# Place of the split weights in on-chip memory, and the order of a few steps, in a two-block transformer kernel

## The reference

```python
u = rms_norm(h, attn_norm[l])
proj = einsum('bsd,dc->bsc', u, w_in[l])          # 7424 columns
dq, dk, dv, rq, rk, rv, rg, gq, gk, gv, gate_logits = split_cols(proj, IN_SPLITS)
lam = exp(sum(lam_q1 * lam_k1)) - exp(sum(lam_q2 * lam_k2)) + lambda_init
a = differential_attention(rope(norm(dq)), rope(norm(dk)), dv, lam)   # 4 heads: softmax - lam * softmax
r = bidirectional_retention(rope(rq), rope(rk), rv, ...)              # 4 heads: scores * decay
c = grouped_query_attention(rope(norm(gq)), rope(norm(gk)), gv)       # 8 query heads, 2 key heads
merged = sum(sigmoid(gate_logits) * stack([a, r, c]) @ w_branch[l])
h = h + merged @ w_out[l]
h = h + square(relu(rms_norm(h) @ w_mlp_in[l])) @ w_mlp_out[l]
```

## Time and profile before

| what | value |
| --- | --- |
| median of 3 runs | 3566.72 us (3562.89 to 3567.04) |
| the profiled execution, its own time | 3565.11 us |
| its span in the trace | 3563.3 us (1.8 us lie around it) |
| granted clock of PE, mean (1.00 is 2.4 GHz) | 0.994 |
| PE busy | 3455.9 us, 97% of the span |
| DVE busy | 1744.8 us, 49% |
| ACT busy | 1377.2 us, 39% |
| transfers of the main queue | 308.18 MB, 30.8% of the DMA engines' span |

### The profile page before, as it was taken

One profiled execution on the slowest core, in us unless ns is written; L12 is line 12 of the kernel. 1 busy time (PEld: TensorE's weight loads), 2 busy tenths in 40 slices (PEclk: granted clock), 3 DMA queues, 4 the chain that ended last, 5 costly groups with the idle time before them and its releaser, 6 DMA issues.

```text
span 3563.3 us, 46888 instructions
## 1 busy us (share of the span) xinstructions
PE 3455.9 (97%) x17777; PEld 2705.9 (76%) x17777; DVE 1744.8 (49%) x2520; ACT 1377.2 (39%) x2048; POOL 6.2 (0%) x13
## 2 busy tenths in 40 slices
PE   8998999999999989999999899999999999999999
PEld 5565788788876657887888776588888886579998
DVE  6675434433466754344434557543323355844334
ACT  5554323322246643233222334533323334543334
POOL 0000000000000000000000000000000000000000
PEclk9999999999999999999999999999999999999999
DMA  4121233555541212335565310022222222023332
GB/s 129 52 67 51 80 97 104 148 159 151 149 104 53 64 51 80 98 111 148 153 179 159 83 56 3 2 60 65 61 64 65 59 74 73 4 58 91 94 94 89
DMA packets 577229, 310.26 MB, mean 87 GB/s; under 512 B 28400, under 2 KB 569024, under 8 KB 577088
## 3 DMA queue, kind: packets, MB, share of 16 engines
q1 hardware_dynamic: 576816, 308.18, 30.8%
q10 hardware_dynamic: 272, 0.13, 0.0%
HBM read 297.26 MB, written 2.10 MB: 84 GB/s over the span
## 4 chain that ended last, share of the span: by engine, by line
PE 90%; DVE 5%; ACT 3%; issue 1%; DMA 1%; SPq 0%; DVEq 0%; ACTq 0%
PE ps L1127 14%; PE ps L1129 14%; PE ps L1128 14%; PE ps L1436 11%; PE ps L1438 10%; PE ps L1440 10%; PE ps L1637 2%; PE ps L1317 2%; PE ps L1286 2%; PE ps L1211 1%; PE ps L1298 1%; PE ps L1571 1%; DVE cacc L2955 1%; PE ps L1314 1%; PE ps L1292 1%
## 5 line engine op out<-in xcount | busy, mean ns | idle before, releaser
L1798 ACT ACTIVATE whi<-wraw 128x1024 fp32r<-128x1024 f32 x448 | 470.7, 1052 | 545.8 <-DMA wraw<-in_w_mlp 245.6
L1127 PE MATMUL ps<-uhi,whi 128*128 128x512 f32 (+1 forms) x1456 | 610.3, 419 | 11.9 <-DVE wlo L2436 4.9
L2436 DVE TENSOR_TENSOR wlo<-wraw,whi 128x1024 fp32r<-128x1024 f32 x448 | 545.8, 1219 | 104.7 <-ACT whi L1798 100.1
L1129 PE MATMUL ps<-uhi,wlo 128*128 128x512 f32 (+1 forms) x1456 | 568.8, 391 | 0.0
L1128 PE MATMUL ps<-ulo,whi 128*128 128x512 f32 (+1 forms) x1456 | 564.8, 388 | 0.0
L1127 PEld LDWEIGHTS ps<-uhi,whi 128*128 128x128 f32 x1456 | 274.1, 188 | 94.7 <-issue 37.8
L1128 PEld LDWEIGHTS ps<-ulo,whi 128*128 128x128 f32 x1456 | 274.3, 188 | 68.4 <-issue 16.3
L1129 PEld LDWEIGHTS ps<-uhi,wlo 128*128 128x128 f32 x1456 | 273.8, 188 | 61.7
L1436 PE MATMUL ps<-u2hi,whi 128*128 128x512 f32 (+1 forms) x1216 | 295.1, 319 | 3.7 <-DVE wlo L2436 2.5
L1436 PE MATMUL ps<-yhi,whi 128*128 128x512 f32 (+1 forms) x976 | 295.9, 354 | 0.0
L1438 PE MATMUL ps<-ylo,whi 128*128 128x512 f32 (+1 forms) x976 | 294.0, 352 | 0.0
(11 more groups left out here) (334 smaller groups left out, 4533.7 us busy)
## 6 DMA issues: line engine op xcount, KB each, us to landing
wraw<-in_w_in SPq DMA_DIRECT2D x128, 512.0 KB, 3.8
wraw<-in_w_mlp SPq DMA_DIRECT2D x128, 512.0 KB, 3.9
mod_raw<-in_w_mod SPq DMA_DIRECT2D x96, 512.0 KB, 5.3
wraw<-in_w_mlp_in SPq DMA_DIRECT2D x64, 512.0 KB, 4.2
wraw<-in_w_mlp_out SPq DMA_DIRECT2D x64, 512.0 KB, 3.9
wraw<-in_w_branch SPq DMA_DIRECT2D x16, 512.0 KB, 3.4
wraw<-in_w_out SPq DMA_DIRECT2D x16, 512.0 KB, 3.8
wraw<-in_w_o SPq DMA_DIRECT2D x16, 512.0 KB, 3.8
```

What stands on the lines that cost most here:

```text
L1127: pe.matmul(bank, whs[:, i], x_hi[:, k], start=(i == 0), stop=False)
L1129: last = pe.matmul(bank, wls[:, i], x_hi[:, k], start=False, stop=(i == n - 1))
L1798: act.activation(whi[:, r], wraw[:, r], ACT.Copy).then_inc(w_hi, 1)
L2436: dve.tensor_tensor(wlo[:, r], wraw[:, r], whi[:, r].bitcast(F32), ALU.subtract).then_inc(w_split, 1)
```

## The change

In words, part by part. **Memory:** the arrays `par_mod` and `ident` are handed out ahead of `whi`, so that `whi` begins at byte 2048 and `wraw`/`wlo` at 18432; every slice then begins at a multiple of 512 and none crosses a line of 2048. From `par_dw` on nothing moves, so the activations stay where they are. **PE at the start:** after the last sum of squares 16 products of `ident` with itself into a bank that is overwritten later. **ACT and DVE at the start:** rounding and splitting of chunk 1 are moved behind the root and into the norm; the lambdas are moved behind chunk 2's split. **Heads:** "attended" stands 0.02 instead of 0.4 behind its attend, which moves `bhi`, `blo`, `fsq` and `fo` ahead of other steps on ACT and DVE, in both layers; and the second turn of a gqa unit goes 0.01 behind the next whole part where that part would cut it (one unit in each layer; on PE 8 turns then stand as 4, six products, 4).

```diff
+            first = at + UNIT_SPACE + 0.05
+            piece = math.floor(first) + 1.01
+            second = piece if first + 0.7 < piece < first + 0.84 else first + 0.7
+            for turn in (first, second)[:2 if kind == "gqa" else 1]:
+                s = put(turn, "turn", score=unit, index=int(turn > first))
+                put(turn + 0.3, "turned", head=s, score=unit, index=s.index)
...
-        put(at + 0.4, "attended", head=att)
+        put(at + 0.02, "attended", head=att)
...
+        par_mod = sb("par_mod", [P, 2 * MOD_COLS])
+        ident = sb("ident", [P, P])
         whi = sb("whi", [P, RAW, 1024], F32R)
...
-        ident = sb("ident", [P, P])
         par = sb("par", [P, P])
...
-        par_mod = sb("par_mod", [P, 2 * MOD_COLS])
...
             pe.sem_inc(norm_summed, 1)
+            pe.wait_ge(h_in, KT)
+            for _ in range(16):
+                pe.matmul(ps[:, 0, 0:P], ident[:, :], ident[:, :], start=True, stop=True)
...
-            for chunk in range(2):
-                weight_hi(chunk)
+            weight_hi(0)
...
                 root_of(n.root, n.aux, D, NORM_EPS, (v_ready, n.v + n.tiles))
-
-                if n.chunk:
-                    act.wait_ge(chunk_done, n.chunk)
+                weight_hi(1)
                 for j in range(n.tiles):
...
+                            if step.chunk == 0:
+                                lambdas()
...
-            for chunk in range(LO_AHEAD):
-                weight_lo(chunk)
+            weight_lo(0)
...
+                    if j == 2:
+                        for chunk in range(1, LO_AHEAD):
+                            weight_lo(chunk)
...
                     if step.name == "lo":
                         lo_before(s.norm1.chunk + step.index)
+                        if l == 0 and step.index == 0:
+                            small_lambdas()
```

More of the change, by code:

```diff
@@ L180, in head_schedule @@
             put(at + 1.7, "weigh", score=unit)
-            for m in range(2 if kind == "gqa" else 1):
-                s = put(at + UNIT_SPACE + 0.05 + 0.7 * m, "turn", score=unit, index=m)
-                put(at + UNIT_SPACE + 0.35 + 0.7 * m, "turned", head=s, score=unit, index=m)
+            first = at + UNIT_SPACE + 0.05
[4 more added lines that the diff above has]
+                put(turn + 0.3, "turned", head=s, score=unit, index=s.index)
         at += UNIT_SPACE + 1.45
         att = put(at, "attend", hd=hd, kind=kind, h=part, layer=layer)
-        put(at + 0.4, "attended", head=att)
+        put(at + 0.02, "attended", head=att)
         if kind == "diff":
@@ L1958, in keep_context, with first_norm @@
                     act.activation(context_squares[:, some], hh[:, some, SEQ:ALL], ACT.Square).then_inc(context_squared, 1)
-            def norm(n, between=None):
+            def first_norm(n):
                 act.wait_ge(norm_summed, n.norm + 1)
                 root_of(n.root, n.aux, D, NORM_EPS, (v_ready, n.v + n.tiles))
-                if n.chunk:
-                    act.wait_ge(chunk_done, n.chunk)
+                weight_hi(1)
                 for j in range(n.tiles):
@@ L1968, in norm @@
                     act.activation(uhi[:, j], vst[:, (n.v + j) % 2], ACT.Copy).then_inc(hi_ready, 1)
-                    if between:
-                        between(j)
             act.wait_ge(sq_used, KT)
@@ L1976, in _ @@
                 else:
-                    norm(s.norm1)
+                    first_norm(s.norm1)
                 if s.layer == 0:
@@ L1980, in _, with lambdas @@
                         weight_hi(chunk)
+                def lambdas():
                     act.wait_ge(par_turned, 3)
@@ L2517, in norm_in_halves, with first_norm @@
                     rest(KT - 1)
-            def norm(n, gain):
+            def first_norm(n, gain):
                 inverse_root(n.root)
@@ L2553, in _ @@
                 else:
-                    norm(s.norm1, ROW["attn_norm"] + KT * l)
-                if l == 0:
+                    first_norm(s.norm1, ROW["attn_norm"] + KT * l)
                     small_parameters()
```

1 line of the change is left out of this document (added).

## The result

The change makes the kernel slower. Its median is 3594.52 us (3590.52 to 3596.01, 4 runs), against 3565.4 us before (4 runs): a ratio of 1.0076, with a 95% interval from 1.0063 to 1.0088. The profiled execution took 3590.52 us. Forecast was 3561, between 3552 and 3569.

The account below looks back on a forecast made before the run. PE, holding 90% of the chain that ended last, was taken as the bound. Terms -3.4 + 5.6 - 6.2 - 1.7 - 0.1 = -5.8 us brought 3566.7 to 3561, range 3552 to 3569.

Parts of the forecast that it names:

- Memory: Weight loads and transfers: moving all slices to one offset gives nothing on PE; taken as 0, at most 5.0 us.
- Rival 2: The new memory places do speed something up, 10.8 us per nanosecond per product: 3545 to 3556; 8 in 100.
- Rival 4: Slower: `blo` blocks DVE at the first and third attends too, costing 17.4 and not 5.6: 3573; 8 in 100.
- the first and third attends: gqa attends where `bhi`, `blo` pass a copy, a weigh and a peak: taken as 0, between -0.5 and +0.5.
- The orders: All moved steps outside memory: the terms of start, attends, clock and split turn, summed to -5.8 us.
- The start: Start of the kernel: earlier root and later lambdas let chunk 2 begin earlier on PE; 3.4 us gained, bounds 2.2 to 3.8.
- the 37.4 that was named: Sign at the start: chunk 2 begins on PE near 37.4, with no lambdas ahead of its split.
- The second gqa attend: Weigh and split wait behind `blo`, making a later turn late: 2.8 us lost per layer, 5.6 in both.
- The fourth attend: Fourth gqa attend: earlier `bhi` and `blo` remove PE's wait for the bank; 3.1 us gained per layer, 6.2 in both.
- The lower clock behind the fourth attend: Layer 1, behind the removed wait: 3.3 us at half clock vanish if the pause causes them; 1.7 us gained.
- rival 3: The fourth attend's gain is given back: DVE or ACT late by 3 us, clock falls elsewhere: 3569; 12 in 100.
- The turn's wait for `gw`: Split second turn of a gqa unit removes one wait for `gw`; 0.1 us gained in all, at most 1.6.

Follow-up runs that it names:

- the orders alone: The changed kernel with the old places in memory, so all reordered steps and the 16 products but no memory part: 3561.64 us, ratio 0.998.

## Why the prediction was wrong

**The step that failed** is "Memory": "the offset doesn't show, so moving all to one offset should give nothing on PE". It was worth +33 us by the trace, and 1.0089 by the memory part alone. Two things were wrong in it. It looked at the length of the loads, 188 ns before and after, while the loss is in the distance between products. And its comparison couldn't show anything: the four old offsets of the slices, 128, 640, 1152 and 1664, are all 128 above a multiple of 512, so all slices stood at one and the same distance (192 modulo 256) from the activations. A slice that crosses a line of 2048 bytes costs nothing: at the same distance `uhi` has 229.5 ns before, where a quarter of the slices cross, and 229.4 with weights and `uhi` both moved, where none does. That part of the step was right, but it was not the question. The transfers did become a little faster, 3.6 and not 3.8 us from issue to landing at the median for `w_in`, and nothing came of it: the second block's wait for `wlo` stays at 2.5 us. The trace of before had a hint: `u2hi`, whose rows of 3104 bytes lie at many distances, had steps of 232.9 ns and the other families 229 to 230.

**Rival 2** had the right mechanism and price (one nanosecond per product is 10.8 us), but was only looked at in one direction, as a gain, and so stood inside no range on the slow side. Rival 4, the slow one, did not occur: the first and third attends cost nothing that can be seen.

**The orders** came out as forecast: -5.8 us, and 0.998 [0.997, 0.999] measured, some 7 us. Term by term:

- The start gained 2.7 us between the two executions above (forecast 3.4), because the split of chunk 2 waited 0.81 us for `lag`; with the orders alone there is no such wait, and over all executions it is 3.7. That chunk 2 began at 37.11, near the 37.4 that was named, is chance, since the input came 1.08 us earlier. The prediction took the 16 products as worth nothing and priced them at 2.6 us; they took 3.73, and where they stand there is no lower clock at the first products any more. The time for chunks 0 and 1 stayed, 12.8 us before and 12.9 after, as the prediction had it, but not for its reason: before they ran in part at half the clock, after they wait for slices.
- The second gqa attend lost 3.15 us in layer 0 (22.17 - 19.02) and 2.8 in layer 1, where 2.8 was forecast for each. None of it is the slower products, as it is 22.16 with the orders alone.
- The fourth attend gained 8.25 - 5.24 = 3.0 us (forecast 3.1).
- The lower clock behind the fourth attend has gone, as forecast. In the nine profiled executions without the attended move it begins within 1.5 us of that wait's end in 12 of 18 places, in layer 0 as well as in layer 1, and in the five with the move in none of 10. So it goes with the wait, though it does not come every time. The prediction counted one place of 1.7 us; 12 of them in nine executions are 2.3 us per execution. In the kernel after, 3.4 us of the lower clock stand behind the second attend of layer 1, which cost 1.7 us; rival 3 had a fall elsewhere as a possibility. With the orders alone and with the attended step alone, which have the same waits, it does not occur there.
- The turn's wait for `gw` only moved, 7.9 + 2.7 us in the two rows before and 6.3 + 4.1 after.

One trace shows less than the sum: with the orders alone the last load of `bhi`'s slices in the first block begins at 1998.0 and not 2001.5, 3.5 us earlier. The second block then runs at the lower clock at places that differ from one execution to the next, so a pair of traces doesn't show the whole: over the executions the terms come to 3.7 - 6.0 + 6.0 + 2.3, some 6 us gained.

**What stays open** is why the distance counts. That the load of a slice and the stream of the activations hinder each other is what a dependence on their distance suggests, since the loads run beside the products; but no run here shows it by itself. Nor is it settled why a change from 512 to 256 columns costs `yhi` some 8 ns at distance 0 and under 2 at 192 and 64, and why products of 256 columns go the other way between distances 192 and 64.

## What to carry to other kernels

Where PE streams products back to back, compare the time from start to start by operand, and try the place of one operand against the other in steps of 32 or 64 bytes: here a bad place cost some 30 us and a better one gave 7, for an edit of one or two lines, and a round number was the wrong guess. Before an offset is called harmless, make sure that the offsets compared really differ in what could count. And an early copy out of a bank helps only if what it is moved past does not have to wait with it: the same edit gained 3 us at the one attend and lost 3 at the other.

## What the runs showed of the hardware

In these runs, at the granted clock of 1.00, products of 512 columns in float32r with a load of 128 x 128 each start 227 to 234 ns apart, and it goes with the distance between the two operands in on-chip memory modulo 256 bytes: 227 to 228 at 0, 229 to 230 at 192, 233 to 234 at the other six distances tried (`yhi`, half of whose products are followed by narrower ones, is 1 to 4 ns off). The load's own length stays at a median of 188 ns at all of them. A pattern goes along with it: before, the three passes are most often 232, 226 and 229 ns apart in turn; after, `bhi`'s commonest steps are 236 and 231 in every pass.

At the start, 4.84 us in which PE was idle were followed by 3.4 us at 1.2 GHz; where 3.73 us of products that nobody uses stood in that pause, the clock stayed at 2.4 GHz.
